# The last part of the second FFN: three down units by seven block products, the fourth by sums of weight blocks

## The reference, cut to what matters

```python
x = x + HALF * gt1 * _swiglu(_rmsnorm(x, g_ffn1) * (1 + sc1) + sh1, w_ffn1_up, w_ffn1_down)
...                                  # token mixers, x = x + gtm * mix
x = x + HALF * gt2 * _swiglu(_rmsnorm(x, g_ffn2) * (1 + sc2) + sh2, w_ffn2_up, w_ffn2_down)
return x, ...                        # and then y = _rmsnorm(x, g_final)

def _swiglu(x, w_up, w_down):
    gu = x @ w_up
    g, u = jnp.split(gu, 2, axis=-1)
    return (jax.nn.silu(g) * u) @ w_down
```

## Time and profile before

| what | value |
|---|---|
| median of 3 runs | 1012.18 us (1011.8 to 1012.29) |
| the profiled execution: its time, its span | 1009.97 us, 1008.2 us |
| TensorE (PE) busy, share of the span | 988.8 us, 98% |
| VectorE (DVE) | 666.3 us, 66% |
| ScalarE (ACT) | 526.0 us, 52% |
| GpSimd (POOL) | 595.2 us, 59% |
| chain that ended last, share on PE | 92% |
| the four down units of the last part, from the chain | 957.67 to about 997.7 us |

### The profile page before, as it was taken

One profiled execution on the slowest core, in us unless ns is written; L12 is line 12 of the kernel. 1 busy time (PEld: TensorE's weight loads), 2 busy tenths in 40 slices (PEclk: granted clock), 3 DMA queues, 4 the chain that ended last, 5 costly groups with the idle time before them and its releaser, 6 DMA issues.

```text
span 1008.2 us, 19940 instructions
## 1 busy us (share of the span) xinstructions
PE 988.8 (98%) x7592; PEld 950.0 (94%) x7592; DVE 666.3 (66%) x1341; ACT 526.0 (52%) x957; POOL 595.2 (59%) x497
## 2 busy tenths in 40 slices
PE   8899999999999999999999999999999999999997
PEld 7799999999999998889977898999999999999996
DVE  3677666676666644469995446976666766766465
ACT  5656554566544552373264436665555665445432
POOL 2267766667666563346877143577666776665642
PEclk9999999999999999999999999999999999999998
DMA  9832322222224327745214622223222322222222
GB/s 361 334 116 84 110 101 85 84 105 106 85 85 153 140 85 290 272 157 200 84 34 180 238 90 79 85 87 122 85 85 85 119 91 84 85 110 100 84 85 95
DMA packets 22716, 127.51 MB, mean 126 GB/s; under 512 B 4192, under 2 KB 7392, under 8 KB 8032
## 3 DMA queue, kind: packets, MB, share of 16 engines
q1 hardware_dynamic: 19744, 105.28, 28.5%
q10 hardware_dynamic: 2880, 20.97, 5.5%
HBM read 123.06 MB, written 3.19 MB: 125 GB/s over the span
## 4 chain that ended last, share of the span: by engine, by line
PE 92%; DVE 3%; POOL 2%; ACT 1%; DMA 1%; issue 1%; DVEq 0%; POOLq 0%; ACTq 0%
PE tile_b L728 22%; PE tile_a L728 22%; PE ada_ps L728 17%; PE tile_a L589 12%; PE tile_b L589 10%; PE ada_ps L561 2%; PE tile_b L611 1%; DMA ada_lo<-w_ada 1%; PE tile_a L886 1%; POOL last_taps L2313 1%; PE stat_ps L815 1%; PE ada_ps L898 1%; PE tile_a L956 1%; DVE x_lo L1604 1%; PE tile_b L648 1%
## 5 line engine op out<-in xcount | busy, mean ns | idle before, releaser
L2169 POOL TENSOR_TENSOR w_lo<-w_raw,w_hi 128x512 fp32r<-128x512 f32 x168 | 216.7, 1296 | 108.8 <-ACT w_hi L1069 108.3
L2169 POOL TENSOR_TENSOR w_lo<-s_raw,w_hi 128x512 fp32r<-128x512 f32 x112 | 146.2, 1307 | 69.0 <-ACT w_hi L1069 69.0
L1069 ACT ACTIVATE w_hi<-w_raw 128x512 fp32r<-128x512 f32 x168 | 104.8, 625 | 64.8 <-PE ada_ps L728 50.2
L2133 POOL TENSOR_TENSOR w_lo<-w_raw,w_hi 128x2048 fp32r<-128x2048 f32 x16 | 73.5, 4596 | 96.8 <-ACT w_hi L1044 93.8
L728 PE MATMUL tile_a<-x_hi,w_hi 128*128 128x288 f32 x400 | 118.7, 297 | 0.0
L728 PE MATMUL tile_b<-x_hi,w_hi 128*128 128x288 f32 x400 | 118.5, 296 | 0.0
L728 PE MATMUL tile_b<-x_lo,w_hi 128*128 128x288 f32 x400 | 118.2, 296 | 0.0
L728 PE MATMUL tile_a<-x_lo,w_hi 128*128 128x288 f32 x400 | 118.2, 296 | 0.0
L728 PE MATMUL tile_a<-x_hi,w_lo 128*128 128x288 f32 x400 | 117.8, 295 | 0.0
L728 PE MATMUL tile_b<-x_hi,w_lo 128*128 128x288 f32 x400 | 117.8, 294 | 0.0
L728 PE MATMUL ada_ps<-x_hi,w_hi 128*128 128x288 f32 x320 | 94.9, 297 | 0.0
(11 more groups left out here) (308 smaller groups left out, 2980.8 us busy)
## 6 DMA issues: line engine op xcount, KB each, us to landing
w_raw<-w_units SPq DMA_DIRECT2D x78, 1024.0 KB, 4.8
ada_lo<-w_ada SPq DMA_DIRECT2D x16, 1024.0 KB, 7.7
ada_lo<-w_ada ACTq DMA_DIRECT2D x14, 1024.0 KB, 7.5
ada_hi<-w_ada ACTq DMA_DIRECT2D x6, 1024.0 KB, 6.1
x<-x_in SPq DMA_DIRECT2D x4, 576.0 KB, 5.5
y_out<-x SPq DMA_DIRECT2D x8, 288.0 KB, 2.5
conv_s<-conv_state SPq DMA_DIRECT2D x1, 480.0 KB, 10.9
conv_s_out<-conv_s SPq DMA_DIRECT2D x1, 480.0 KB, 4.3
```

What stands on the lines that cost most here:

```text
L1069: nc.scalar.activation(slot(w_hi, i), source, ACT.Copy).then_inc(ready, 1)
L2133: nc.gpsimd.tensor_tensor(w_lo[:, side, :], w_raw[:, side, :], w_hi[:, side, :].bitcast(F32), ALU.subtract).then_inc(w_lo_ready, 1)
L2169: return nc.gpsimd.tensor_tensor(slot(w_lo, i), raw, slot(w_hi, i).bitcast(F32), ALU.subtract)
```

## The change

The fast downs now reach into the last part of the second FFN: `FAST_DOWNS` says for each FFN and part how many downs are fast, (4, 4, 0) and (4, 4, 3). In a fast down of that part a block row is 3 x 128 = 384 wide instead of 512 (`wide(u)`, `k_blocks(u)`), so a product is 9 matmuls. Since its downs need them, the six up units of that part now make the T sums of their hidden chunks.

The fourth down has no B12 any more (T4 stands there). For the second token half it uses A11+A12 and A21+A22 (`u_sums`, split by `u_high` and `u_low`) with B22, and A11 and A21 with T3; it still makes 72 matmuls, tile_b first now. `last_down_window`, `last_down_sums` and the POOL block place this work: the squares of x and the split of the fourth unit's weights now stand in the window of the third fast down.

```diff
 FAST_PARTS = 2
+FAST_DOWNS = ((DOWNS, DOWNS, 0), (DOWNS, DOWNS, DOWNS - 1))
...
-            for i in range(PLAIN_UPS if part == 0 else 0, n + (DOWNS if part < FAST_PARTS else 0)):
+            for i in range(PLAIN_UPS if part == 0 else 0, n + FAST_DOWNS[f][part]):
...
-    return u in FAST and not is_down(u) and UNIT_KIND[u][1] < FAST_PARTS
+    return u in FAST and not is_down(u) and FAST_DOWNS[UNIT_KIND[u][0]][UNIT_KIND[u][1]] > 0
...
+            def last_down_product(ps, t, h, k, n):
+                if h and k % 2:
+                    ws, cols = (u_block(u_hi, t), u_block(u_lo, t)), slice(k // 2 * P, (k // 2 + 1) * P)
+                else:
+                    ws, cols = (w_hi[:, 0], w_lo[:, 0]), slice(up_block(t, k) * P, (up_block(t, k) + 1) * P)
+                s = ((X_B11, X_B21), (X_T3, X_B22))[h][k % 2]
...
+            def last_down_unit(u, n):
+                pe.wait_ge(w_lo_half, half_before(u) + 1)
...
+                for h in range(2):
+                    if h:
+                        pe.wait_ge(u_lo_ready, 1)
+                    for k in range(n):
+                        mm = last_down_product(tile_b, 0, h, k, n)
...
-                for k in range(KH):
+                kc = k_blocks(u)
+                for k in range(kc):
...
-                    for i in range(DOWNS):
-                        down_unit(down + i, n, before + n, None, 3 if i == DOWNS - 1 else None)
+                    last_down_unit(down + DOWNS - 1, n)
...
+            def last_down_window(u, down):          # ACT
+                hi_a22(u)
+                copy_p1(u)
+                square(3, 0)
+                square(3, 1)
+                split_hi_half(down, 0)
+                u_high(0)
+                u_high(1)
+                split_hi_half(down, 1)
+                scale_c22(u)
+                square(3, 2)
...
+            def u_sums(u):                          # DVE
...
+                nc.vector.tensor_tensor(s3_raw[:, 0:n], quarter(u, A11, n), quarter(u, A12, n), ALU.add).then_inc(u_sum, 1)
...
+            def last_down_sums(u, down):
+                add_c21_c12(u - 1)
+                residual_pair(u - 1)
+                u_sums(down)
+                add_p15(u)
+                add_u2(u)
+                add_square(3, 1)
+                add_c22(u)
+                residual_c11(u)
+                add_square(3, 2)
+                add_square(3, 3)
+                add_c21_c12(u)
+                residual_pair(u)
+                add_square(3, 4)
+                add_square(3, 5)
+                residual(down, KD - 2, 1, 2 * (KD - 1), GATE[2])
+                add_square(3, 6)
+                last_residual(down, 3, GATE[2])
...
+                    down += DOWNS - 1               # POOL
+                    split_lo_half(down, 0)
+                    u_low(0)
+                    split_lo_half(down, 1)
+                    residual_c22(down - 1)
+                    u_low(1)
```

More of the change, by code:

```diff
@@ L99 @@
 FAST = {u: o for o, u in enumerate(UNIT_KIND)}
-FAST_OF_FFN = len(FAST) // 2
+FAST_OF_FFN = sum(kind[0] == 0 for kind in UNIT_KIND.values())
 FIRST_FAST = (FFN1 + PLAIN_UPS, FFN2 + PLAIN_UPS)
@@ L107 @@
 PAIRS_OF_FFN = FAST_PARTS * PAIRS_OF_PART
-DOWNS_OF_FFN = FAST_PARTS * DOWNS
+DOWNS_OF_FFN = sum(FAST_DOWNS[0])
 def is_down(u):
@@ L138, in has_sums, with k_blocks, wide @@
 def has_sums(u):
-    return u in FAST and not is_down(u) and UNIT_KIND[u][1] < FAST_PARTS
+    return u in FAST and not is_down(u) and FAST_DOWNS[UNIT_KIND[u][0]][UNIT_KIND[u][1]] > 0
+def k_blocks(u):
+    return FF_PARTS[LAST_PART] // 2 if is_down(u) and UNIT_KIND[u][1] == LAST_PART else KH
+def wide(u):
+    return P * k_blocks(u)
 def downs_before(u):
@@ L645, in final_tile @@
                             final_spread(0, stat_ps).then_inc(r_ready, 1)
[L646 to L650, removed]
+                        mm = last_down_product(tile_a, 1, h, k, n)
+                    mm.then_inc((tile_half_done, tile_done[0])[h], 1)
             def final_fillers(count):
@@ L728, in product @@
                         mm = pe.matmul(ps, slot(w, i)[:, P * k:P * (k + 1)], r,
-                                       start=(first and n == 0 and k == 0), stop=(n == 2 and k == KH - 1),
+                                       start=(first and n == 0 and k == 0), stop=(n == 2 and k == kc - 1),
                                        skip_group_check=not first)
@@ L757, in fast_unit @@
                 hidden = f * sum(FF_PARTS) + sum(FF_PARTS[:part + 1])
-                pairs = 4 * (f * PAIRS_OF_FFN + (part + 1) * PAIRS_OF_PART)
+                pairs = 4 * (f * PAIRS_OF_FFN + sum(FF_PARTS[:part + 1]) // 2)
                 pe.wait_ge(s_lo_pool, 4 * o + 1)
@@ L2357, in column_units, with ffn_units @@
         if by_quarter:
-            both = np.concatenate([blocks[0::2, :, a], blocks[1::2, :, a], blocks[1::2, :, b], blocks[0::2, :, b]])
+            for q, part in enumerate((blocks[0::2, :, a], blocks[1::2, :, a], blocks[1::2, :, b], blocks[0::2, :, b])):
+                out[n, :, QUARTER * q:QUARTER * q + k // 2 * P] = part.transpose(1, 0, 2).reshape(P, k // 2 * P)
         else:
             both = np.concatenate([blocks[:, :, a], blocks[:, :, b]])
-        out[n, :, :2 * k * P] = both.transpose(1, 0, 2).reshape(P, 2 * k * P)
+            out[n, :, :2 * k * P] = both.transpose(1, 0, 2).reshape(P, 2 * k * P)
     return out
-def ffn_units(up, down):
+def ffn_units(up, down, fast_downs):
     import numpy as np
@@ L2369, in ffn_units @@
     pairs_out = [(m, m + 1) for m in range(0, KD, 2)]
-    for n in FF_PARTS:
+    for n, fast in zip(FF_PARTS, fast_downs):
         units.append(column_units(up, [(f, n_hidden + f) for f in range(first, first + n)]))
-        units.append(column_units(down[first * P:(first + n) * P], pairs_out, by_quarter=(n == KD)))
+        units.append(column_units(down[first * P:(first + n) * P], pairs_out, by_quarter=(fast > 0)))
         first += n
```

141 lines of the change are left out of this document (94 added, 47 removed).

## The result

The kernel after takes 1015.17 us (median of 19 runs, 1009.58 to 1018.42), the kernel before 1011.33 in the 19 runs beside them. The ratio is **1.0030 (95%: 1.0020 to 1.0039)**, so 3.0 us slower (the two medians lie 3.8 us apart), where I had forecast +0.8 and "no change". The median lies above my range of 1010.3 to 1014.4. The profiled execution took 1013.09 us and lies inside it; its span is 1011.2.

What follows compares the result with a forecast made beforehand. The prediction took TensorE (PE), busy for 98% of the span, to bound the kernel. Its terms, -3.57 + 2.0 + 0.5 + 1.9 = +0.8 us, put the median of 1012.18 at 1013.0, range 1010.3 to 1014.4.

Steps and rivals of the forecast that it cites:

- What is removed: Last part's downs: 261 matmuls instead of 288; the 27 that go, at 0.1322 each, give -3.57 us.
- T sums at nothing: Six ups of the last part: the T sums they now make are hidden and cost nothing.
- The opening, +2.0: Last part's first fast down: PE waits for POOL's `h_lo` and DVE's `full`, 2.01 us lost; bounds 0.70 and 2.3.
- DVE against POOL in the third fast down, +0.5: DVE additions with both inputs in SBUF wait out POOL's running instruction, delaying PE by 0.5 us; bounds 0 and 2.4.
- Strict blocking: Rival: between DVE and POOL, a second instruction starts only when the first has ended; +1.8, 1014.0 us; chance 0.10.
- Fourth unit, +1.9: Fourth unit and final norm: late DVE makes PE wait for residual, sums of squares and half square; +1.9 us, bounds 0 and 3.
- "What follows the last tile is the same work": Behind the last tile: the work is the same as before, so no difference was counted there.
- Sum: Whole kernel: -3.57 + 2.0 + 0.5 + 1.9 = +0.8 us, 1013.0 on the median, "no change".
- the case of a half split ahead of weight sum 2: Rival, third fast down: DVE waits 2.40 us more for POOL, `add_u2` about 2.1 late; +2.7, 1014.9 us; chance 0.15.
- The main case: Whole kernel: all counted terms hold, +0.8 us, 1013.0; own range 1012.2 to 1013.8; chance 0.50.

Runs made afterwards that it cites:

- Experiment 3: Kernel after with DVE's `add_u2` ahead of the two weight sums in the last part's first fast down: 1013.47 us, ratio 1.0012.
- experiment 9: Kernel after with the fourth unit's two POOL half splits of 1024 columns cut into four of 512: 1015.48 us, ratio 1.0037.
- experiment 4: Kernel before with four additional DVE subtractions of 576 columns ahead of the residual of chunk 6, making PE wait in the last tile: 1018.86 us, ratio 1.0066.
- experiment 5: Kernel before with four additional DVE subtractions ahead of chunk 6's residual, plus thirteen and four PE transposes in the last tile's two waits: 1013.54 us, ratio 1.0020.
- experiment 1: Kernel after with eight and four extra PE transposes ahead of the two waits of the last tile: 1013.81 us, ratio 1.0011.
- experiment 7: Kernel after with `add_u2` ahead of the weight sums at all five openings of fast downs: 1013.00 us, ratio 1.0011.
- experiment 2: Kernel after with DVE's additions of squares in the third fast down moved behind `add_c22` and the pair residual: 1014.32 us, ratio 1.0018.
- experiment 11: Kernel after with transposes ahead of the last tile's waits, later additions of squares, and early `add_u2` at all five openings: 1008.25 us, ratio 0.9965.
- experiment 8: Kernel before with `add_u2` ahead of the weight sums at its four openings of fast downs: 1009.67 us, ratio 0.9984.
- experiment 12: Kernel before with early `add_u2` at its four openings and eight and four transposes in its last tile: 1010.36 us, ratio 0.9989.

## Where the prediction was right and where it was wrong, by its steps

- **What is removed**: right. The second fast down takes 8.34 us from start to start, just 63 x 0.1324; nothing in it waits.
- **T sums at nothing**: right. From the first fast unit to the first down of the last part it is 893.25 and 893.26 us in the two profiles after, 893.43 before.
- **The opening, +2.0**: 10.28 - 8.34 = 1.94, at the two waits that were named (the profile gives them 0.73 and 0.70, where I had about 1.0 and 0.9; measured from start to start the two cost the whole 1.94). Experiment 3 took the second away and gained 0.82.
- **DVE against POOL in the third fast down, +0.5**: 8.76 - 8.34 = 0.42, and L2044, L1640 and the first of L1643 took 1.37, 2.23 and 2.33, ending 0.41 to 0.62 behind POOL's instructions. The Trainium skill, "SBUF — State Buffer", section "SBUF: two separate sides", says that whichever of the two engines starts first gets the shared pair "for the whole instruction"; experiment 9 agrees, with 2.23 becoming 1.12 when that instruction was halved. Strict blocking fell: L1640 ended 0.61 behind the split, not 0.76.
- **Fourth unit, +1.9**: 13.20 - 11.32 = 1.88, and by starts the parts are nearly mine. Its first tile takes 4.94 us against 36 x 0.1322 = 4.76, 0.18 more (I had 0.15). From the second tile to the sums of squares it is 4.71 against 3.58, 1.13 more (1.1). From there to the half square it is 1.13 against 0.59, 0.54 more (0.8 - 0.3 = 0.5). The 0.15 for restarts is part of these distances. The waits that the profile names, 0.90 and 0.29, are shorter than these distances.
- **"What follows the last tile is the same work"**: this step failed. It is the same work, and I put its difference at nothing. Before, it ran at a granted clock of 1.00 until 1000; after, at 0.50 from 998 on, and it took 2.57 us more. The prediction counted what PE's idle time in the last tile costs by its length alone, and had no term for the clock. Experiments 4 and 5 show what it missed: one and the same delay costs 6.7 us with PE idle and 2.0 with PE busy. In experiment 1, the transposes took 1.5 us off the part behind the last matmul of this profile and nothing off the part before.
- **Sum**: +0.8 was +0.7 from the opening to the last matmul. With the 2.57, and 0.27 less ahead of the opening, it is 3.0 on the span (3.12 on the profiled time), as the ratio has it. With no more than +0.8 on the median, the time would have been in my range; the missing term took it out.
- **Rivals**: the case of a half split ahead of weight sum 2 gave nearly the right time, 1014.9, and by a mechanism that didn't occur: POOL's first split starts at 979.82, when the second weight sum (978.59 to 979.96) is at its end. A right number by a wrong way. The main case had the right mechanisms in front of the last matmul. The step with the clock is in none of the rivals.

Not settled: why the clock falls in one execution and not in another. In every profile it falls below 1.00 before the span ends, in that of before too (0.83 at 1000 to 1002, then 0.50); what differs is how early. With waits of 0.8 to 0.9 and 0.3 it fell to 0.50 in two profiles of after, in experiment 7 and (0.6 and 0.3) in experiment 2, and held until at least 1000 in experiments 3 and 9. It also fell in experiment 11 from 1000 on, 2.6 us behind the last matmul, and in experiment 8 (0.86 at 996 to 998, the last matmul at 994.92), both without a wait in the last tile. So the waits make an early fall likely, not certain; what that costs is known as a mean only, from the ratios. The median clock of all executions is 0.988 and 0.989 in the two timings of after and 0.991 for the kernel before.

Not ruled out either: a part of the 3.0 us that arises at the start. The first fast unit begins at 63.2 to 66.2 us in the five profiles of before and its variants, and at 63.7 to 68.1 in the nine of after and its variants (means 64.3 and 66.2). Nothing of the change lies ahead of it, and in the two profiles compared above it begins at 64.07 and 63.98, so it has no share in their difference; but no run here separates it from chance in the ratios. Experiments 4 and 5 are both variants of before and their profiles start alike (63.98 and 64.09), so what they show of the clock doesn't hang on it.

Of the change's 3.57 us, some 1.9 to 2.4 remain once its stalls are mended (0.9965 against 0.9984 and 0.9989 for before with like edits, intervals that overlap a little): that it is worth something is likely, its size is loose.

## What to carry to other kernels

A wait of PE can cost more than its length when the work behind it is short and on the path (6.7 us for waits worth 2.5 in experiments 4 and 5): read the clock column of the windows behind the wait that a change will make, and price the work there at either level. When PE must wait near the end, give it something harmless to do, and only there: in experiment 12, where it doesn't wait, that gained nothing. When a unit gets narrower, the chains that don't shrink with it (here the hidden sums in front of `add_u2`) come due earlier; put what PE waits for ahead of what only the next unit needs.

## What was not expected of the hardware

- The granted clock went from 1.00 to 0.50 behind two waits of 0.90 and 0.29 us, 30 us after the last wait of any such length (963.88). The Trainium skill, "TensorE: Matmul & The Clock Gate", section "HAM oscillation — how this bites in real kernels", tells of a clock that falls in PE's waits for DMA, longer ones than those here. The trace agrees in that the fall comes behind waits, and differs in that it came behind waits this short, and with the same waits in some executions and not in others.
- One and the same kernel differs between executions by the clock: after ran from 1009.58 to 1018.42 us. In the first 50 us, with a DMA share of 0.89 to 0.90, the granted clock is 0.97 in the profiles of before and after and 0.90 in the second of after, and its first fast unit starts at 66.2 us instead of 64.0. These 2.2 us are most of the 3.0 that were to be told, so a single run says nothing here.
